# Layer 0's experts: 128 of 512 tokens by gathered rows of their chosen experts, v's low halves on GpSimd

## What is computed

```python
q = (t @ w_query).reshape(t_count, PEER_HEADS, 2, PEER_HALF)
s = jnp.einsum('thpd,hpkd->thpk', q, sub_keys).astype(F32)
s1, i1 = lax.top_k(s[:, :, 0], PEER_TOPK)
s2, i2 = lax.top_k(s[:, :, 1], PEER_TOPK)
...
top_s, pos = lax.top_k(cand_s, PEER_TOPK)
idx = jnp.take_along_axis(cand_i, pos, axis=-1).reshape(t_count, PEER_HEADS * PEER_TOPK)
gate = jax.nn.softmax(top_s, axis=-1).reshape(t_count, PEER_HEADS * PEER_TOPK).astype(h.dtype)
...
act = jax.nn.gelu(jnp.einsum('pkd,pd->pk', expert_u[ib], tb), approximate=False) * gb
return jnp.einsum('pk,pkd->pd', act, expert_v[ib])
```

## Time and profile before

| | |
|---|---|
| median of 3 runs | 3962.04 us (3956.68 to 3964.13) |
| span of the profiled execution | 3967.1 us |
| TensorE busy | 3777.8 us, 95% |
| VectorE busy | 2641.8 us, 67% |
| ScalarE busy | 1589.2 us, 40% |
| GpSimd busy | 980.6 us, 25% |
| moved by DMA | 650.53 MB, mean 164 GB/s |
| mean granted TensorE clock | 0.967 of full speed |

### The profile page before, as it was taken

How to read it: one execution, slowest core, us unless ns; L and a number is a source line. 1 busy time by engine, 2 the same in 40 slices (tenths; PEclk the granted TensorE clock), 3 DMA queues, 4 the chain that set the end, 5 groups by cost and what they waited for, 6 DMA issues and landing times.

```text
span 3967.1 us, 60163 instructions
## 1 busy us (share of the span) xinstructions
PE 3777.8 (95%) x24424; PEld 3307.4 (83%) x24424; DVE 2641.8 (67%) x5092; ACT 1589.2 (40%) x2370; POOL 980.6 (25%) x476
## 2 busy tenths in 40 slices
PE   7998999999999999999999999999999999988899
PEld 5667998888888888778888888699999999978799
DVE  3794554389677777367766665778773777766575
ACT  2323444333344444322111213644665333447454
POOL 1334454234433333300000000067666000000000
PEclk8989999899999999999999998999999999998899
DMA  5240000224445554676776753057778788742255
GB/s 190 100 138 22 1 1 1 59 90 139 141 162 184 183 180 166 229 237 231 256 241 232 244 181 91 20 169 216 236 259 272 245 270 275 230 157 86 86 170 170
DMA packets 222723, 650.53 MB, mean 164 GB/s; under 512 B 20080, under 2 KB 89584, under 8 KB 214640
## 3 DMA queue, kind: packets, MB, share of 16 engines
q1 hardware_dynamic: 116224, 401.92, 32.2%
q10 hardware_dynamic: 106224, 244.77, 17.2%
HBM read 544.38 MB, written 101.71 MB: 163 GB/s over the span
## 4 chain that ended last, share of the span: by engine, by line
PE 83%; DVE 7%; ACT 4%; DMA 3%; issue 1%; POOL 1%; ACTq 0%; POOLq 0%; SPq 0%; DVEq 0%
PE ps L133 82%; PE ps L136 2%; DVE lo L80 1%; DMA ring<-in_v 1%; ACT hi L128 1%; DVE g_b L80 1%; POOL lo L80 1%; DMA ring<-in_gdn_in 1%; ACT L124 1%; DVE cond L113 0%; DMA ring<-in_u 0%; ACTq L75 0%; ACT n_s L125 0%; DMA pcA<-pcga 0%; DVE g_acc L92 0%
## 5 line engine op out<-in xcount | busy, mean ns | idle before, releaser
L80 POOL TENSOR_TENSOR lo<-ring,hi 128x1024 fp32r<-128x1024 f32 x328 | 800.0, 2444 | 1905.9 <-ACT hi L128 1905.8
L128 ACT ACTIVATE hi<-ring 128x1024 fp32r<-128x1024 f32 x725 | 767.9, 1060 | 1093.3 <-PE ps L133 816.7
L80 DVE TENSOR_TENSOR lo<-ring,hi 128x1024 fp32r<-128x1024 f32 (+1 forms) x397 | 486.6, 1227 | 314.6 <-ACT hi L128 313.9
L133 PE MATMUL ps<-pahh,hi 128*128 128x512 f32 x1152 | 464.3, 403 | 12.3 <-POOL lo L80 9.4
L133 PE MATMUL ps<-pahh,lo 128*128 128x512 f32 x1152 | 452.1, 392 | 0.0
L133 PE MATMUL ps<-pahl,hi 128*128 128x512 f32 x1152 | 452.1, 392 | 0.0
L80 DVE TENSOR_TENSOR paone<-ps,paR 128x512 bf16<-128x512 f32 x512 | 329.3, 686 | 145.9 <-PE ps L133 141.5
L133 PE MATMUL ps<-pchh,hi 128*128 128x256 f32 x1152 | 334.6, 290 | 16.4 <-POOL lo L80 14.6
L133 PE MATMUL ps<-pchl,hi 128*128 128x256 f32 x1152 | 326.7, 284 | 0.0
L133 PE MATMUL ps<-pchh,lo 128*128 128x256 f32 x1152 | 326.5, 283 | 0.0
L133 PEld LDWEIGHTS ps<-pahh,hi 128*128 128x128 f32 x1152 | 218.4, 190 | 54.5 <-POOL lo L80 10.4
(11 more groups left out here) (455 smaller groups left out, 9142.3 us busy)
## 6 DMA issues: line engine op xcount, KB each, us to landing
ring<-in_u SPq DMA_DIRECT2D x256, 512.0 KB, 3.7
ring<-in_v SPq DMA_DIRECT2D x256, 512.0 KB, 4.3
paA<-paga ACTq DMA_DIRECT2D x128, 256.0 KB, 2.8
paG<-paR ACTq DMA_DIRECT2D x16, 2048.0 KB, 7.9
paAg<-paA ACTq DMA_DIRECT2D x16, 2048.0 KB, 8.6
paGg<-paG ACTq DMA_DIRECT2D x16, 2048.0 KB, 16.9
late_w<-in_adat ACTq DMA_DIRECT2D x56, 512.0 KB, 3.8
ring<-in_ffn_up SPq DMA_DIRECT2D x44, 512.0 KB, 3.9
```

The costliest lines, as they stand in the source:

```text
L80: return Op(self.e.tensor_tensor(out, a, b, op) if self.real else None)
L128: return Op(self.e.activation(out, a, ACT.Copy, scale=scale) if self.real else None)
L133: return Op(self.e.matmul(out, l, r, start=start, stop=stop, skip_group_check=skip) if self.real else None)
```

## The change

Layer 0's PEER is now `peer_first`, with `first_up` and `first_down` in place of `peer_up` and `peer_down`; layer 1 keeps `peer`.

- Tokens 0 to 383 stay dense: products of 384 columns, 96 gate groups, spills and gates three quarters as large. Tokens 384 to 511 (token tile T = 3) go by rows.
- VectorE routes tiles 3 and 0 first, decodes tile 3 (`rows_chosen`) into `paidx`, the expert number of each token's 128 choices, and then routes tiles 1 and 2.
- GpSimd issues 256 indirect DMAs (`gather`), 128 of u rows and 128 of v rows; each brings one row of 1024 fp32 to each of 128 partitions, 512 KB, into one of six buffers (`parow`). Each waits until the buffer's last row was used. They stand between the low halves in GpSimd's order.
- The 128 tokens' activations are turned by TensorE into PSUM banks 2 and 3 (`wide`, 16 products). For each u row VectorE takes a dot with `wide` (128 dots); ScalarE and VectorE then make Gelu times gate (`pacoef`). For each v row VectorE adds row times coefficient to one of two sums (`paacc`, 128 operations), and at the last v tile TensorE turns the two sums into the output banks (16 products).
- Since banks 2 and 3 are taken, the gate groups have all operands in SBUF: 16 TENSOR_SCALARs of 128x128 in bf16 a group in place of five TENSOR_TENSORs of 128x512. The decoding takes its comparison numbers from SBUF.
- Transposition is at tile 46, and the groups start at tile 50, one, one and two a tile.
- v's low halves of layer 0 are on GpSimd. In the down pass ScalarE, not VectorE, makes the activations' high half. Late dots have three tile buffers in place of four and run one step earlier.

The diff, cut to its core:

```diff
+ROWS = 6
...
+        name = stream[i][0]
+        if name[0] == "v":
+            return s_lo_pool if name[1] == 0 else s_lo_dve
+        return s_lo_pool if name[0] in ("gdn_in", "gdn_out", "wq", "u") else s_lo_dve
...
-    split = {"hi": 0, "lo": 0}
+    split = {"hi": 0, s_lo_dve: 0, s_lo_pool: 0}
...
-    def lo_to(i, last=None):
-        while split["lo"] < min(rank[i] + AHEAD, len(splits)):
-            t = splits[split["lo"]]
+    def lo_to(i, last=None, own=None):
+        own = own or lo_signal(i)
+        e = dve if own is s_lo_dve else pool
+        while split[own] < min(rank[i] + AHEAD, len(splits)):
+            t = splits[split[own]]
             if t > i + REACH or last is not None and t > last:
                 break
-            split["lo"] += 1
+            split[own] += 1
+            if lo_signal(t) is not own:
+                continue
             k, w = pair_of[t], stream[t][2]
-            e = dve if lo_signal(t) is s_lo_dve else pool
             e.wait_ge(s_hi, t)
-            e.tt(lo[:, k, 0:w], slots[slot(t)][:, 0:w], hi[:, k, 0:w].bitcast(F32), SUB).then_inc(lo_signal(t), t)
+            e.tt(lo[:, k, 0:w], slots[slot(t)][:, 0:w], hi[:, k, 0:w].bitcast(F32), SUB).then_inc(own, t)
...
+        def gather(r):
+            if r == 0:
+                pool.wait_ge(S("picked"), ("pa", "rows"))
+            if r >= ROWS:
+                q = r - ROWS
+                if q < 128:
+                    pool.wait_ge(s_dot, q)
+                else:
+                    pool.wait_ge(s_add, q - 128)
+            pool.gather(row[r % ROWS][:, :], u_rows if r < 128 else v_rows, idx[:, r % 128:r % 128 + 1]).then_inc(
+                s_row[r % ROWS], r, 16)
+        def dot(k):
+            if k == 0:
+                dve.wait_ge(S("route_turned"), ("pa", "h"))
+            if k >= 2:
+                dve.wait_ge(s_dot, k - 2)
+            dve.wait_ge(s_row[k % ROWS], k)
+            dve.dot(junk[k % 2], row[k % ROWS][:, :], wide[:, :], dots[:, k:k + 1]).then_inc(s_dot, k)
+        def add(k):
+            r = 128 + k
+            x, c = sparse["sums"][k % 2], coef[:, k:k + 1]
+            dve.wait_ge(s_row[r % ROWS], r)
+            if k < 2:
+                dve.ts(x, row[r % ROWS][:, :], c, None, MUL).then_inc(s_add, k)
+            else:
+                dve.wait_ge(s_add, k - 2)
+                dve.stt(x, row[r % ROWS][:, :], c, x, MUL, ADD).then_inc(s_add, k)
...
+        turn_at, start = 46, 50
+        spread = (1, 1, 2)
+        many = {i: spread[i % len(spread)] for i in range(start, 128)}
...
+        dots_head = {hh: range(3 * hh - 6, 3 * hh - 3) for hh in range(2, 8)}
+        dots_unit = {j: [18 + j] for j in range(8)}
+        dots_group = {g: [26 + g] for g in range(n_groups)}
+        dots_group[n_groups - 1] = range(25 + n_groups, 128)
...
+            i = 14 + r if r < ROWS else min(due_at[r - ROWS] + 1, 127)
...
+            for c in range(8):
+                for x in range(2):
+                    op = pe.mm(wide[:, c * 128:(c + 1) * 128], h[x][:, c, wd:w].bitcast(F32), ident, x == 0, x == 1)
+            op.then_inc(s_turn, (name, "h"))
+            match(15)
...
+                    op = pe.mm3(ps[:, 0:wd], (x[0][:, cs], x[1][:, cs]), (h[0][:, c, 0:wd], h[1][:, c, 0:wd]), c == 0, c == 7)
...
+        def rows_chosen():
+            x = tv[:, T]
+            dve.cp(top3, x[:, :, 0]).then_inc(s_pick, (name, "top rows"))
+            dve.cp(ixf[:, T], ixu[:, T]).then_inc(s_pick, (name, "ixf rows"))
+            dve.wait_ge(s_pick, (name, "top rows"))
+            dve.tt(x, x, bc(top3.unsqueeze(2), (128, 8, 16)), SUB).then_inc(s_pick, (name, "shifted rows"))
+            bits("rows", tiu[:, T].rearrange("p h k -> p (h k)"), abu[:, 0:128], ap3)
+            decode("rows", [(T, q) for q in range(2)], (eqs[0], eqs[3]), lambda t, q: ap3[q], lambda t, q: sel3[q])
+            dve.stt(ap3[0], sel3[0], 128.0, sel3[1], MUL, ADD).then_inc(s_pick, (name, "numbers"))
+            dve.wait_ge(s_pick, (name, "numbers"))
+            dve.cp(sparse["idx"][:, :], ap3[0]).then_inc(s_pick, (name, "rows"))
+            softmax_sum("rows", (name, "rows"), x, sum3, sparse["gate"][:, :].rearrange("p (h k) -> p h k", h=8), 8).then_inc(
+                s_pick, (name, "row gates"))
...
+            for hh in range(8):
+                dve.wait_ge(s_q, (name, "score", 2 * hh + 1))
+                route(hh, (T, 0))
+            rows_chosen()
+            for hh in range(8):
+                route(hh, (1, 2))
+                for k in dots_head.get(hh, ()):
+                    dot(k)
...
+            for g in range(n_groups):
+                o = one[g % 3]
+                if g >= 3:
+                    dve.wait_ge(s_mm, (name, g - 3))
+                for t in range(4):
+                    c = slice(4 * g + t, 4 * g + t + 1)
+                    dve.ts(o[:, 0, t], iota_b, I2[:, c], None, ALU.is_equal)
+                    for a in range(3):
+                        op = dve.ts(o[:, 1 + a, t], iota_b, I1[:, c], GP[a][:, c], ALU.is_equal, MUL)
+                op.then_inc(s_both, (name, g))
+                for k in dots_group[g]:
+                    dot(k)
...
+            for i in range(128):
+                lo_to(u[i], u[127])
+                for r in fetched.get(i, ()):
+                    gather(r)
...
+        added = {i: range(i * 128 // 124, (i + 1) * 128 // 124) for i in range(124)}
+        fetched = {}
+        for r in range(128, 256):
+            i = 0 if r < 128 + ROWS else min(next(j for j in added if r - 128 - ROWS in added[j]) + 1, 127)
+            fetched.setdefault(i, []).append(r)
...
+                    op = pe.mm3(bank[m][:, 0:wd], (x[0][:, cs], x[1][:, cs]), r, i == 0, i == 127, skip=True)
+                    if i == 127:
+                        if m == 7:
+                            op.then_inc(s_used, v[i])
+                        if m == 0:
+                            pe.wait_ge(s_add, 127)
+                        for j in range(2):
+                            op = pe.mm(bank[m][:, wd:w], sparse["sums"][j][:, cs], ident, j == 0, j == 1, skip=True)
+                        op.then_inc(s_last, (name, m))
...
+            for i in range(128):
+                hi_to(v[i])
+                if i == 0:
+                    high(0)
+                if i < 127:
+                    high(i + 1)
+                if i == 2:
+                    sparse["factor"](3)
+                late[0](i)
...
+            def gated(i):
+                k = i // 8
+                if i % 8 == 0:
+                    dve.wait_ge(s_ag[k % 2], (name, k))
+                    dve.wait_ge(s_gg[k % 2], (name, k))
+                x = Ag[k % 2][:, i % 8, :].rearrange("p (b t) -> p b t", t=32)
+                dve.tt(x, x, Gg[k % 2][:, :, i % 8, :], MUL).then_inc(s_gated, i)
+            def low(i):
+                dve.wait_ge(s_high, i)
+                dve.tt(av[i % 2][1][:, :], Ag[(i // 8) % 2][:, i % 8, :], av[i % 2][0][:, :].bitcast(F32), SUB).then_inc(
+                    s_act, (name, i))
+            lo_to(v[0], v[0])
+            gated(0)
+            gated(1)
+            low(0)
+            for i in range(128):
+                if i < 126:
+                    gated(i + 2)
+                if i < 127:
+                    low(i + 1)
+                lo_to(v[i], v[127], s_lo_dve)
+                if i == 4:
+                    sparse["row_factor"](3)
+                if i == 0:
+                    dve.wait_ge(s_coef, 2)
+                if i == 100:
+                    dve.wait_ge(s_coef, 3)
+                for k in added.get(i, ()):
+                    add(k)
+                late[1](i)
...
-    peer(0, 0, 512, "pa", ("s1", 0, None), late=True)
+    peer_first()
```

More of the change, by code:

```diff
@@ L116, in drop8, with gather @@
         return Op(self.e.match_replace(out, top, a, -3e38) if self.real else None)
+    def gather(self, out, table, index):
+        if not self.real:
+            return Op(None)
+        return Op(self.e.indirect_dma_start(out, None, table, bass.IndirectOffsetOnAxis(ap=index, axis=0)))
 class Act(Queue):
@@ L310, in program, with issue @@
             with ExitStack() as st:
-                issue(nc, d, mem, signals, bank, real, st)
-def issue(nc, d, mem, S, bank, real, ctx):
+                issue(nc, d, mem, signals, bank, wide, real, st)
+def issue(nc, d, mem, S, bank, wide, real, ctx):
     pe = Pe(nc.tensor, real)
@@ new lines, in sparse_rows @@
+    def sparse_rows(sparse):
+        s_row = [S(f"row_loaded{i}") for i in range(ROWS)]
+        s_dot, s_add = S("row_dot"), S("row_added")
+        row, idx, dots, coef = (sparse[n] for n in ("row", "idx", "dots", "coef"))
+        u_rows = d["u_rows"]
+        v_rows = d["v"][0].rearrange("i p n -> (i p) n")
+        junk = [x.bitcast(BF16) for x in n_sq]
+        sums = mem.over("paacc", [128, 2048], "n_rs")
+        sparse["sums"] = [sums[:, 1024 * i:1024 * i + 1024] for i in range(2)]
+        def gather(r):
```

(10 more changed lines are left out.)

409 lines of the change are left out of this document (399 added, 10 removed).

## The result

The changed kernel takes **3984.1 us** (median of 4 runs, 3977.05 to 3989.03), the kernel before beside it 3959.4 (3952.27 to 3964.13). The ratio is 1.0059, its 95% interval 1.0041 to 1.0078: slower by 0.6%. The profiled execution of after spans 3987.7 us, that of before 3967.1. Executions of one kernel differ by 12 us here, in one experiment by 29. Each profile is of one execution, so lengths read from two profiles can differ by some microseconds for no cause.

The account below looks back on a forecast made before the run. VectorE, taking turns with GpSimd over SBUF, was to bound both passes: 3967.1 + 29 (v's start) - 12 (v) + 2 (last products) = 3986, less 5.1 to the median gives 3981 us; range 3820 to 4110.

Parts of the forecast that it names:

- What bounds it next: Both passes: VectorE and GpSimd can't work at once on SBUF inputs, so each low half costs VectorE a 2.2 us turn.
- Rival B: Both passes: no turns for these forms, gate loop bound by TensorE, v takes 529 us; 3596 us in all, chance 0.06.
- Rival C: Gate loop: gathers keep VectorE's short fast operations out, 115 us at 1.2 us each; 4096 us in all, chance 0.29.
- Rival A: Gate loop: low halves mostly fall beside dots, hiding 110 of 158 us, second scalar free; 3838 us in all, chance 0.22.
- TensorE's saving: Both passes: products of 384 columns at 0.172 us, saving 335 us over 256 tiles, and 21 us from fewer gate groups.
- Tile 46: Up pass before the gates: TensorE waits there some 22 us for VectorE's routing and choosing; first group at 1127.
- A group's operations: Gate loop on VectorE: 16 x 0.173 us and a 1.15 us dot, 3.92 us a group, 376 for 96; second scalars 33.
- Turns: Gate loop: each of 72 low halves delays VectorE's one-hot operations by 2.2 us, 158 us in all.
- The handover: From last gate group to v: six tiles (25 us) and 5 us, v's start at 1724, 29 us later than before.
- The down pass: v: VectorE's turns and work of 5.54, 4.96 and 4.39 us a tile, 654 us, then 687; 12 us less than before.
- The 5% for a tighter chain: v: allowance taken between 0 and 10% for high halves waiting on ScalarE and late loads, raising 654 to 687 us.
- The clock: TensorE: the forecast is wrong if the granted clock falls below 1.00 through the many short pauses.

Follow-up runs that it names:

- experiment 2: Changed kernel with the gate loop's numbers 0 to 127 read as fp32 from a PSUM bank, not bf16 from SBUF: 3989.1 us, ratio 1.0069.
- experiment 1: Changed kernel with v's low halves of layer 0 back on VectorE: 3933.6 us, ratio 0.9928 to the kernel before.
- experiment 10: Changed kernel with the constant 0.5 in place of the gate, a second per-partition scalar, in 12 operations a group: 3888.9 us.
- experiment 8: Changed kernel with v's low halves on VectorE, five-operation gate groups, and the second activations-and-gates group loaded after the last spill: 3741.3 us, ratio 0.9471.
- experiment 9: Changed kernel with the second group of activations and gates loaded after the last spill: 3990.1 us, ratio 1.0069.
- experiment 12: Kernel before the change with only the second group of activations and gates loaded after the last spill: 3939.8 us, ratio 0.9950.
- experiment 7: Changed kernel with v's low halves on VectorE and 122 of 128 gathers of v rows left out: 3867.9 us.
- experiment 11: Changed kernel with the gate loop's numbers 0 to 127 as fp32 in SBUF in place of bf16: 4064.8 us.

## Why the prediction came out right, and what in it was wrong

3981 was forecast and 3984 measured, both slower by over 0.2%, and the mechanism of the forecast held. But that the sum is right to 3 us is luck, since errors cancel: of +20.6 us in the profiled execution (+19 forecast) v's start holds 31 more than forecast, and v and the rest 29 less. The part up to the next stage came out at +43.7, for +19.

- **What bounds it next: right.** VectorE by its turns with GpSimd, in both passes: 581.96 of 582 us, no turns from PSUM (experiment 2), v 72 us shorter without them (experiment 1). Rival B is out. Rival C is out too: a gather lasts 1.04 us in the mean for u and 1.16 for v, and the short operations' starts are not further apart beside it. Six gathers last 2.76 to 2.83 us, over the 2.4 that I named as a sign of being wrong, but they lie in the decoding, beside VectorE's passes of 128x2048. Rival A is out: in the changed kernel all 72 low halves meet a one-hot operation and none falls beside a dot alone. The dot covers part of some turns in experiment 10, worth 25 us.
- **TensorE's saving: right.** 384 columns follow after 0.174 us, for 0.172. Tile 46: the first group came at 1134.7, for 1127, and TensorE was idle for 21 of the 235 us up to it, for 22, but over several waits and not at tile 46 alone.
- **A group's operations: two errors that half cancel.** One-scalar operations cost 0.165 us, not 0.173, but a second pointer costs its full 0.056: 64 us where I took half of 0.06, 33. Turns: 1.6 us a group are 153 us, for 158. The loop ended 22 us late, 8 of them from its start. (The 5.5 us a group among the signs left the second pointer out; the sum itself has 5.9, and 6.06 was measured.)
- **The handover: a misread row, then a term too small.** I took the earlier trace rows's piece, starting at 1695.02, for v; its first product is an up tile's. v began at 1703.08, so the handover cost 13 us before, not 5. After, the way from the last gates to v took 46.1 us, for six tiles (25) and 5. The cause is not a stuck issue alone but the order: store, wait for its landing, 6 MB of loads, a spill behind them. Experiments 8, 9 and 12 take 7 to 13 us of it away. v's start is +59.6, for +29.
- **The down pass: mechanism right, size nearly.** -15.9 us with its tail, for -10. Turns were 2.1 us a tile, for 2.2. The 5% for a tighter chain was a guess, and no run prices it by itself. That the transfers stood right behind was in the sum (691 us) and is borne out by experiments 1 and 7, but not at that length: 309 GB/s was no ceiling, 351 are held over 200 us, which is 4.9 us a tile, and v took 628.6 us.
- **The clock:** I named falling below 1.00 as a way to be wrong. It fell to 0.91 in the loop. VectorE filled the loop, 581.96 of 582 us, and its length is explained without the clock.
- **The rest: taken as 0, was -23.1 us, and is mostly no effect.** The same code after v takes 1524.1 to 1547.2 us in the 14 profiled executions of these kernels; after has the shortest and before the longest. Part of it is the granted clock: over the rest it was 0.959 in the mean in before's execution and 0.965 in after's, 127 and 108 us at the lower level, which is some 10 us by an estimate that counts the lower level as half the work. The three executions from the kernel before (1547.2, 1544.0, 1538.2) lie above most of the others (mean 1533), so some of the remainder may be real. That stays open.

## What to carry to other kernels

Cutting the bound engine's work pays only up to the next engine: write down the next one's microseconds a tile, including what each operand's place costs it, and the transfers' behind it. A rewrite forced by a lost buffer or bank (here 16 operations from SBUF for five with an operand in PSUM) can cost more than the idea gains; look for the bank elsewhere first: two product banks for four gave back 166 us and, with the low halves on VectorE, made the same idea 5% faster than the kernel before. And check by its operand names what the first and last instruction of a piece of the chain are, before its start is taken for a stage's start.

## What the hardware showed that I had not expected

- A TENSOR_SCALAR of 128x128 costs by distance of starts 0.163 us (bf16 from SBUF, changed kernel), 0.198 (fp32 from SBUF, experiment 11), 0.26 (fp32 from PSUM, experiment 2) with one pointer scalar, and 0.06 more with two. A second step with a constant costs nothing (0.163, experiment 10).
- A VectorE operation with data from PSUM and pointer scalars from SBUF does not wait for GpSimd's subtraction of two SBUF operands (at most 0.43 us, experiment 2); with its data in SBUF, fp32 or bf16, it does, for up to 2.2 us.
- A gather of 128 rows of 4 KB holds GpSimd for 0.94 us at the least (mean 1.04 for u, 1.16 for v). It can have to wait for VectorE: beside a 128x2048 pass with SBUF inputs that ran from 1103.43 to 1105.71, the gather that started at 1103.79 took 2.76 us. 256 of them moved 134 MB beside the other queues.
- Transfers of these sizes reached 374 GB/s over 205 us in experiment 8, with the DMA engines 0.99 busy; the highest stretch read before showed 309.
- Transfers that are queued can hold the engine that issues them: in experiment 1's v 13 of ScalarE's issues of late tiles took 7.2 to 10.4 us each, one about every 40 us, where its other 70 issues mean 0.36.
- In after's gate loop, where the granted clock is 0.91 in the mean, TensorE paused 3.55 us before the gate products at 1698.85; from 1700.36 to 1704 its products were 0.32 us apart, the lower of its two levels (1.2 GHz), and then 0.174 again (2.4 GHz). Products of after's timeline on either side:

```profile
1702.28 0.52 PE L139 MATMUL ps<-pahl,hi 128*128 128x384 f32 x1
1702.60 0.52 PE L139 MATMUL ps<-pahh,lo 128*128 128x384 f32 x1
...
1704.68 0.33 PE L139 MATMUL ps<-pahh,hi 128*128 128x384 f32 x1
1704.85 0.33 PE L139 MATMUL ps<-pahl,hi 128*128 128x384 f32 x1
```
